# Where a row of modulation values is multiplied: chunks on TensorE, or on Pool and ScalarE with one sum on TensorE

## The reference

```python
cond = jax.nn.silu(c)
for l in range(DEPTH):
    mod = cond @ ada_w[l] + ada_b[l]                 # (1, 1024) @ (1024, 6144)
    sh1, sc1, g1, sh2, sc2, g2 = jnp.split(mod, 6, axis=-1)
    h = modulate(rms_norm(x, mix_norm_g[l]), sh1, sc1)
    x = x + g1[:, None, :] * token_mixer(h, ...)     # projections, convolution, scan, pooling, attention
    h = modulate(rms_norm(x, ffn_norm_g[l]), sh2, sc2)
    x = x + g2[:, None, :] * peer_ffn(h, ...)        # 16 query tiles, top-16 search, experts u and v
```

## Time and profile before

| | us |
|---|---|
| median of 3 runs | 2915.8 |
| lowest and highest | 2914.14, 2917.41 |
| the profiled execution, its own time | 2911.22 |
| its span | 2909.4 |
| PE busy | 2849.5 |
| DVE busy | 2501.1 |
| ACT busy | 1446.6 |
| POOL busy | 996.6 |

### The profile page before, as it was taken

How to read it: one execution, slowest core, us unless ns; L and a number is a source line. 1 busy time by engine, 2 the same in 40 slices (tenths; PEclk the granted TensorE clock), 3 DMA queues, 4 the chain that set the end, 5 groups by cost and what they waited for, 6 DMA issues and landing times.

```text
span 2909.4 us, 48871 instructions
## 1 busy us (share of the span) xinstructions
PE 2849.5 (98%) x17734; PEld 2665.6 (92%) x17734; DVE 2501.1 (86%) x4773; ACT 1446.6 (50%) x2309; POOL 996.6 (34%) x773
## 2 busy tenths in 40 slices
PE   6999999999999999999999999999999999999998
PEld 4777789999999999999978778999999999999998
DVE  4667789799897899999987779998999879999998
ACT  3345234488883433433353532447888633333333
POOL 1000027644443343444400000675444433443442
PEclk9999999999999999999999999999999999999999
DMA  7434647899999999999932122679999999999996
GB/s 276 170 115 185 255 148 240 304 364 380 387 334 382 346 383 383 383 377 384 380 117 73 63 69 88 199 239 354 391 377 372 348 378 357 384 379 385 377 380 251
DMA packets 252523, 854.87 MB, mean 294 GB/s; under 512 B 25568, under 2 KB 58592, under 8 KB 245728
## 3 DMA queue, kind: packets, MB, share of 16 engines
q1 hardware_dynamic: 149280, 442.23, 41.7%
q0 software_dynamic: 98496, 381.73, 35.0%
q10 hardware_dynamic: 4608, 29.36, 2.4%
HBM read 777.06 MB, written 76.15 MB: 293 GB/s over the span
## 4 chain that ended last, share of the span: by engine, by line
PE 80%; DMA 8%; DVE 7%; ACT 3%; issue 2%; SPq 0%; POOL 0%; DVEq 0%; ACTq 0%
PE banks L1049 40%; PE banks L1565 27%; DMA w_raw<-wst 4%; PE banks L1533 4%; DMA ring<-u,gidx 2%; DVE w_lo L1605 2%; PE banks L1370 2%; ACT w_hi L767 1%; PE banks L1114 1%; PE banks L1453 1%; DMA pj<-adaw 1%; DVE ring L2099 1%; PE banks L1065 1%; DVE oneh L2121 1%; DVE vacc L2111 1%
## 5 line engine op out<-in xcount | busy, mean ns | idle before, releaser
L767 ACT ACTIVATE w_hi<-w_raw 128x1024 fp32r<-128x1024 f32 x596 | 630.7, 1058 | 754.4 <-PE banks L1049 637.6
L1049 PE MATMUL banks<-hH,w_hi 128*128 128x352 f32 (+1 forms) x2528 | 865.5, 342 | 3.4 <-ACT w_hi L767 0.9
L1605 DVE TENSOR_TENSOR w_lo<-w_raw,w_hi 128x1024 fp32r<-128x1024 f32 x522 | 638.8, 1224 | 263.2 <-ACT w_hi L767 260.6
L1049 PE MATMUL banks<-hH,w_lo 128*128 128x352 f32 (+1 forms) x2528 | 845.2, 334 | 0.0
L1049 PE MATMUL banks<-hL,w_hi 128*128 128x352 f32 (+1 forms) x2528 | 844.9, 334 | 0.0
L720 POOL DMA_INDIRECT ring<-v,gidx x320 | 396.2, 1238 | 595.8 <-DVE vacc L2111 533.5
L720 POOL DMA_INDIRECT ring<-u,gidx x320 | 396.8, 1240 | 461.6 <-DVE gact L2099 444.6
L1049 PEld LDWEIGHTS banks<-hH,w_hi 128*128 128x128 f32 x2528 | 474.8, 188 | 50.1 <-issue 20.4
L1565 PE MATMUL banks<-c_lo_late,w_hi 128*128 128x352 f32 x1536 | 494.0, 322 | 0.0
L1049 PEld LDWEIGHTS banks<-hH,w_lo 128*128 128x128 f32 x2528 | 474.4, 188 | 19.5
L1049 PEld LDWEIGHTS banks<-hL,w_hi 128*128 128x128 f32 x2528 | 475.2, 188 | 17.4 <-issue 0.5
(11 more groups left out here) (347 smaller groups left out, 3991.8 us busy)
## 6 DMA issues: line engine op xcount, KB each, us to landing
w_raw<-wst SPq DMA_DIRECT2D x596, 512.0 KB, 6.5
activations<-act_out SPq DMA_DIRECT2D x124, 352.0 KB, 8.0
act_in<-activations SPq DMA_DIRECT2D x62, 704.0 KB, 8.0
gate_matrices<-stages ACTq DMA_DIRECT2D x32, 896.0 KB, 9.2
gates<-gate_matrices SPq DMA_DIRECT2D x64, 448.0 KB, 10.0
ada_buf<-adaw POOLq DMA_DIRECT2D x24, 1024.0 KB, 6.8
nrm<-adaw POOLq DMA_DIRECT2D x8, 1024.0 KB, 5.4
pj<-adaw POOLq DMA_DIRECT2D x7, 1024.0 KB, 7.6
```

Of the source, the lines that this page charges most:

```text
L767: nc.scalar.activation(w_hi[g % 2][:, :, :].rearrange("p a b -> p (a b)"), w_raw[:, g % RAWS, :], ACT.Copy).then_inc(s_wh, 1)
L1049: last = mm(bank[s][:, 0:t.stop - t.start], a[s][:, k, :], b[:, k, t], start=(k == 0 and a is w_hi and b is hH), stop=(k == KT - 1 and a i ...
L1605: v.tensor_tensor(w_lo[g % 2][:, :, :].rearrange("p a b -> p (a b)"), w_raw[:, g % RAWS, :], w_hi[g % 2][:, :, :].rearrange("p a b -> p (a ...
```

## The change

POOL multiplies a chunk by `cond` in place, one value a partition (`scale_ada`, 128x2048), and adds it to the set's first chunk in place (`add_ada`, 128x2048). After seven adds PE sums the set's accumulator over the partitions once, with `ones` as the stationary operand (`ada_sum`, four matmuls as in one `ada_chunk`). This holds for sets 1 and 2 of layer 0 (chunks 8 to 23). Of layer 1's first set, five chunks (24 to 28) stay on PE as before, 29 and 30 are scaled by POOL, and 31 is scaled by ACT. All later chunks (32 to 47) are scaled by ACT in the query tiles, two behind each of the first two tiles and one behind each later one, and added by POOL. Set 0 of layer 0 stays as it is.

The sums stand behind projections 7 and 16 in the mixer, behind scores 3 and 9 in the query tiles, and behind the last scores, after the first u tile. The chunks get new places (`ADA_HOMES`), and a load now waits for an add of POOL's own. POOL waits once for the time-step groups (behind chunk 12, since chunk 16 lies in `h32`) and once for the first sum (behind chunk 17). Two other engines get a new wait: ACT before it copies projection 14 to `pj` (chunk 22 added), and DVE before the first scan result goes to `y_tok` (chunk 17 added).

```diff
+POOL_SCALED = ADA_CHUNKS + GAP_ADA + 2
+def scaled_in(n):
+    return [m for m in range(POOL_SCALED, 2 * ADA_CHUNKS)][2 * n:2 * n + 2] if n < 2 else \
+        [m for m in range(POOL_SCALED, 2 * ADA_CHUNKS)][n + 2:n + 3]
...
+            def scale_ada(n):
+                pool.wait_ge(*ada_sem(n))
+                pool.tensor_scalar(ada_place(n), ada_place(n), tiny[:, 0, n % KT:n % KT + 1], None, ALU.mult).then_inc(s_psc, 1)
+            def add_ada(n):
+                pool.wait_ge(*ada_scaled(n))
+                pool.wait_ge(*(ada_scaled(n - 1) if n - 1 == ada_head(n // KT) else ada_added(n - 1)))
+                acc = ada_place(ada_head(n // KT))
+                pool.tensor_tensor(acc, ada_place(n), acc, ALU.add).then_inc(s_adas, 1)
+            pool.wait_ge(s_cond, 1)
+            pool.wait_ge(s_rows, 1)
+            load_ada(8)
+            pool.wait_ge(s_adat, KT)
+            load_ada(9)
+            load_ada(10)
+            scale_ada(8)
+            for n in range(9, 15):
+                scale_ada(n)
+                add_ada(n)
+                if n == 12:
                     pool.wait_ge(s_dtg, 1)
+                    load_ada(16)
+                load_ada(n + 2 if n < 14 else 17, after=n)
+            scale_ada(15)
+            add_ada(15)
+            load_ada(18, after=15)
+            scale_ada(16)
+            for n in range(17, ADA_CHUNKS):
+                scale_ada(n)
+                add_ada(n)
+                if n == 17:
+                    pool.wait_ge(s_adat, ADA_TAKEN[1])
+                    load_ada(19)
+                elif n + 2 < ADA_CHUNKS:
+                    load_ada(n + 2, after=n)
...
+                    for n in range(ADA_CHUNKS, POOL_SCALED):
+                        load_ada(n)
+                    scale_ada(POOL_SCALED - 2)
+                    scale_ada(POOL_SCALED - 1)
+                    add_ada(POOL_SCALED - 1)
...
+                    for i, n in enumerate(loads):
+                        add_ada(n)
...
+                    if l == 0 and n == N_IN - 4:
+                        act.wait_ge(*ada_added(22))
                     tile_copy(n)
...
+                    for m in scaled_in(n) if l == 0 else []:
+                        act.wait_ge(*ada_sem(m))
+                        nc.scalar.activation(ada_place(m), ada_place(m), ACT.Copy,
+                                             scale=tiny[:, 0, m % KT:m % KT + 1]).then_inc(s_asc, 1)
...
+                def ada_sum(at, i):
+                    n = at * ADA_SETS + i
+                    if at == 0:
+                        pe.wait_ge(s_arow, i)
+                    pe.wait_ge(*ada_added(n * KT + KT - 1))
+                    acc = ada_place(ada_head(n))
+                    for j in range(ADA_GROUPS):
+                        last = mm(bank[ADA_BANK[at][i]][32 * j:32 * j + 32, :], ones[:, 0:32], acc[:, j * T:(j + 1) * T],
+                                  start=(ADA_ON_PE[n] == 0), stop=True)
                     last.then_inc(s_adat, 1)
...
                 for n in range(2, N_IN):
                     project(l, n, n % 2)
-                    if l == 0 and n != KT + 1:
-                        ada_chunk(0, KT + n - 1 if n <= KT else KT + n - 2)
+                    if l == 0 and n in (7, 16):
+                        ada_sum(0, n // 7)
...
                     if l == 0:
-                        for c in chunks_of(n):
-                            ada_chunk(1, c)
+                        if n in (3, 9):
+                            ada_sum(1, n // 9)
...
+                if l == 0:
+                    ada_sum(1, 2)
...
                     dve.wait_ge(s_y, l * NT + tt + 1)
+                    if l == 0 and tt == 0:
+                        dve.wait_ge(*ada_added(17))
```

More of the change, by code:

```diff
@@ L170, with pool_owned, ada_head, scaled @@
 PAIR_K = 5
-def chunks_of(n):
-    return [GAP_ADA + 2 * n, GAP_ADA + 2 * n + 1] if n < 4 else [n + 9]
-assert [c for n in range(N_Q - 1) for c in chunks_of(n)] == list(range(GAP_ADA, ADA_CHUNKS))
+ADA_HOMES = ("nrm", "last_rows", "y_tok", "last_rows", "y_tok", "last_rows", "y_tok", "last_rows",
+             "h32", "y_tok", "last_rows", "nrm", "last_rows", "nrm", "last_rows", "nrm",
[3 rows of a table added]
+assert KT + len(ADA_HOMES) == 2 * ADA_CHUNKS
+ADA_ON_PE = (KT, 0, 0, GAP_ADA, 0, 0)
+POOL_SCALED = ADA_CHUNKS + GAP_ADA + 2
+def pool_owned(n):
+    return n % KT >= ADA_ON_PE[n // KT]
+def ada_head(i):
+    return i * KT + ADA_ON_PE[i]
+def scaled(n):
+    first = KT if n < POOL_SCALED else POOL_SCALED
+    return sum(pool_owned(m) for m in range(first, n + 1))
+ADA_TAKEN = [KT]
+for _i in range(1, 2 * ADA_SETS):
+    ADA_TAKEN.append(ADA_TAKEN[-1] + ADA_ON_PE[_i] + 1)
+def scaled_in(n):
+    return [m for m in range(POOL_SCALED, 2 * ADA_CHUNKS)][2 * n:2 * n + 2] if n < 2 else \
+        [m for m in range(POOL_SCALED, 2 * ADA_CHUNKS)][n + 2:n + 3]
+assert [m for n in range(N_Q - 1) for m in scaled_in(n)] == list(range(POOL_SCALED, 2 * ADA_CHUNKS))
 Y_BANK = (3, 4, 5, 2)
@@ L263, in ada_place @@
         def ada_place(n):
[L265 to L270, removed]
+            rows = lambda r: pj[:, r:r + 4, :].rearrange("p a t -> p (a t)")[:, 0:ADA_COLS]
+            if n < 3:
+                return ada_buf[:, n, :]
             if n < 6:
@@ L571, in ada_sem, with ada_scaled, ada_added @@
                 return s_ada0[n], 16
[L572 to L576, removed]
+            home = ADA_HOMES[n - KT]
+            return s_ada[home], 16 * len([m for m in range(KT, n + 1) if ADA_HOMES[m - KT] == home])
+        def ada_scaled(n):
+            return (s_psc if n < POOL_SCALED else s_asc), scaled(n)
+        def ada_added(n):
+            heads = [ada_head(i) for i in range(1, 2 * ADA_SETS)]
+            count = lambda first: len([m for m in range(first, n + 1) if pool_owned(m) and m not in heads])
+            return s_adas, count(KT)
         block = ctx.enter_context(nc.Block())
@@ L700, in _, with load_ada @@
-            for c in range(KT, ADA_CHUNKS):
-                load_ada(0, c)
+            def load_ada(n, after=None):
+                if after is not None:
+                    pool.wait_ge(*ada_added(after))
+                pool.dma_start(ada_place(n), adaw[n // ADA_CHUNKS, n % ADA_CHUNKS]).then_inc(ada_sem(n)[0], 16)
+            def scale_ada(n):
+                pool.wait_ge(*ada_sem(n))
+                pool.tensor_scalar(ada_place(n), ada_place(n), tiny[:, 0, n % KT:n % KT + 1], None, ALU.mult).then_inc(s_psc, 1)
@@ L796, in ada_rows @@
                 n = at * ADA_SETS + i
-                act.wait_ge(s_adat, n * KT + KT)
+                act.wait_ge(s_adat, ADA_TAKEN[n])
                 if n >= 2:
@@ L1106, in ada_chunk @@
                     i, k = c // KT, c % KT
-                    if at == 0 and i >= 1 and k == 0:
-                        pe.wait_ge(s_arow, i)
-                    first, final = 0, KT - 1
+                    first, final = 0, KT
                     if n < KT:
```

53 lines of the change are left out of this document (29 added, 24 removed), and 3 rows, old and new, of the table ADA_HOMES.

## The result

The changed kernel takes 3028.4 us (median of 4 runs, 3024.6 to 3031.0); the kernel before took 2916.5 beside it (2914.1 to 2917.4). The ratio is 1.0386, 95% interval 1.0371 to 1.0400: 112 us slower, where 3002 were predicted (2910 to 3060). The parts of the sum were not: the mixer cost much more than forecast, the query tiles nothing.

What follows compares the result with a forecast made beforehand. TensorE, busy 98% of the span, was taken to bound the kernel. Mixer +61, before the query tiles +5 and query tiles +20 gave +86 on 2911.2: 2997, or 3002 with the median's 4.6; range 2910 to 3060.

Steps and rivals of the forecast that it cites:

- What bounds the kernel, and who waits: TensorE bounds the kernel; VectorE operations reading two SBUF tensors or copying SBUF to SBUF wait out Pool's operation.
- What TensorE gains: Chunks taken off TensorE: 11.7 us in the mixer, about 18 in the query tiles, 30 if all else were hidden.
- The mixer, +61: First layer's mixer: VectorE held by Pool's scalings and adds, 26 + 21 + 20, less 6 for TensorE's chunks.
- my three pieces: Mixer stretches: chunk 8 to the time-step wait, on to chunk 17, chunks 18 to 23; losses 26, 21, 20 us.
- The granted clock, costed at nothing: TensorE's clock may fall in the mixer's longer pauses, but tiles wait for VectorE anyway: 0 us.
- Before the query tiles, +5: Two scalings and an add, 10.8 us of Pool, meet the second normalisation; half counted, bounds 0 and 10.
- The query tiles, +20: 14 first-layer query tiles at 9.3 us each, 130 us against 110.4; bounds -18 and +42.
- the CAST meets the next add: Query tiles: VectorE's CAST, after a held w_lo, is held 4.3 us by Pool's next add, so VectorE falls behind TensorE.
- The waits and the DMA, at nothing: ScalarE's wait for chunk 22, VectorE's for chunk 17, and the same 48 MB loaded to other places: 0 us.
- Pool waits: Rival: Pool is held instead and TensorE waits at the sums; about +16 us, 2932; chance 0.13.
- Holds hidden: Rival: VectorE's holds are short and fall into waits, so the change is faster, 2891 us; chance 0.13.
- One for one: Rival: every Pool operation holds VectorE and lets one operation by; +140 us, 3056; chance 0.12.

Runs made afterwards that it cites:

- extra_read: Kernel before plus 32 idle Pool subtractions of 128x1024, which read SBUF, in the second layer's mixer: 2954.4 us, ratio 1.0134.
- extra_write: Kernel before plus 60 idle Pool memsets of 128x1024, which only write, in the second layer's mixer: 2923.6 us, ratio 1.0031.
- one_column: Changed kernel with Pool's scalings and adds cut to one column of 2048, loads, waits and sums kept: 2886.0 us, ratio 0.9894.
- early_loads: Changed kernel with the query tiles' first three loads ahead of Pool's two scalings and add, and chunk 32 scaled a tile later: 3022.8 us, ratio 1.0363.
- query_only: Kernel before with the new scheme for chunks 32 to 47 only, in the query tiles: 2923.8 us, ratio 1.0035.
- query_paced3: Kernel before, new scheme for chunks 32 to 47 only, mostly one a tile, adds waiting for VectorE's CAST, last add early enough: 2902.6 us, ratio 0.9965.
- quarters: Changed kernel with each Pool operation of 2048 columns split into four of 512, the same work: 2981.7 us, ratio 1.0236.

## Why the prediction was right, and where it was wrong

**What bounds the kernel, and who waits.** Right. The rows of Pool and VectorE side by side carried it: hL, w_lo, the convolution, even tensor_scalar operations 32 wide (4.3 and 4.5 us in the mixer) are held for a Pool operation. extra_read and extra_write show that for operations with two SBUF inputs it is Pool's reads; a one-input tensor_scalar, as the eight additions are, is held by Pool's writes as well.

**What TensorE gains.** Right: 30 us forecast, 30 measured in one_column; in the mixer 12.9 for 11.7, and in the query stage 15.6 for 18. In the sum I had counted only 6 for the mixer.

**The mixer, +61, measured +97.4.** The mechanism was right and two sizes were off. The scaling, taken at 3.0 us from the affine_select row, costs 5.45 and lies outside my own upper bound, 4.8, because I took one input to be at most as dear as two. That makes 154 us of Pool for 115. And a microsecond of Pool costs 0.71 us, not the 67 / 115 = 0.58 of my three pieces. In numbers: 39 x 0.58 = 23 us by the price, 154 x 0.13 = 20 by the share, and 7 less since TensorE's chunks gave 12.9 and not 6; 61 + 23 + 20 - 7 = 97. The split in price and share is a way of counting; by pieces the tiles become later by 38, 29 and 31 us (conversions at 96.86, 164.20 and 279.03 against 59.07, 97.51 and 181.61 before), where the forecast had 26, 21 and 20 less TensorE's 6. The first two lie above their own upper bounds, 31 and 26. The share was too low since I let Pool's time fall on VectorE's idle time in proportion. Once VectorE is the late one, that idle time is gone (107 of 112 us busy); Pool, with its next operations ready, leaves 0.1 to 0.9 us between them and pauses only at its two waits for TensorE. That this is why the share was too low is argued from the trace; the price, 0.71, is measured.

**The granted clock, costed at nothing.** It fell to 0.59 to 0.79 in the mixer. That the tiles wait for VectorE in any case is argued from its 107 busy us of 112; no run separates the clock from the holds, and 0.71 includes whatever it costs.

**Before the query tiles, +5, measured +19.6.** 10.4 us lie between the output tiles' last conversion and the query stage's first (25.0 for 14.5). That is just over my upper bound of 10; the two scalings take 11.3 us there and not 6. 7.4 more are a step that I missed: the loads of the query stage stand behind Pool's add, and ScalarE's scaling waits for them with the conversion queued behind it. I had named ScalarE's waits in the mixer and not this one. early_loads gives the 7.4 back, 5.8 of them net. The last 1.8 lie in the output tiles.

**The query tiles, +20, measured -4.6.** The step that failed is "the CAST meets the next add". In the steady tiles the add starts 3.5 us after the conversion, as forecast (471.34 and 474.87), but the CAST comes 2.1 us after it and not 4, so that it gets by, and w_lo alone is held. The tile takes 7.56 us and not 9.3. The step does come true where adds queue up: in three tiles of the changed kernel and in four of query_only. query_paced3 shows that a wait can rule it out (its longest CAST is 0.20 us). So the 9.3 us tile was an error of timing, not of mechanism.

**The waits and the DMA, at nothing.** Right for the change as it is: in the mixer of its trace nobody waits for Pool, and the DMA share is 0.24 to 0.37 in the windows above. In quarters one of the two waits lasts 17 us.

**The rivals.** Pool waits: not here, but in quarters. Holds hidden: refuted by the same run that shows the gain. One for one was nearest in the mixer, and for its reason; its query tiles were not. That the total came within 26 us of the forecast, and inside the range, was in part luck: two parts were too low by 36 and 15 us, and the third too high by 25.

**The signs.** VectorE's long operations, the unchanged second layer and the add came as named. The mixer's stretch took 209 us (70.09 to 279.03) for "near 170", the steady query tiles 7.56 for 8 to 11, the longest CAST 3.9 for 4.8, the scaling 5.45 for 3.

## What to carry to other kernels

Before work is moved to Pool, list VectorE's instructions in that stretch that read two SBUF tensors, copy from SBUF to SBUF or are a tensor_scalar on SBUF. Count each long Pool instruction that reads SBUF as time taken from VectorE (here 0.6 to 0.7 us for each us of 2048-wide ones); beside a tensor_scalar count one that only writes, too. Only what lies beside PSUM readers or real idle time is free, and a wait can put it there, as query_paced3 did. Never price one instruction form by another: measure tensor_scalar and tensor_tensor on the engine itself. And where a load is issued by the engine that computes, look at what stands ahead of it in that queue.

## Not expected of the hardware

- On Pool a tensor_scalar over 128x2048 float32 takes 5.45 us, with a column or a constant as its operand; a tensor_tensor of two such tiles 4.55; a tensor_tensor with a broadcast column 3.6 to 3.7.
- Pool is held as well, which the prediction had left open: a scaling that starts at 188.91, while a w_lo is running (until 189.05), takes 6.54 us, and VectorE gets a sum of 1.25 us (188.97) in at full speed.
- Pool's memset (0.99 us for 128x1024) does not hold VectorE's two-input operations, but does hold its tensor_scalar.
- In 512-wide pieces Pool's work is longer (191 us for 154) and costs 0.37 us a microsecond in place of 0.71, two waits for Pool (28.1 and 17.0 us) included.
